# ScalarE sets up the two tap accumulators of a depthwise convolution; one tap fewer takes the product path

## What is computed

```python
def conv_module(u, buf, w_in, w_dw, b_dw, g_ln, b_ln, w_out):
    a, gl, z = jnp.split(u @ w_in, 3, axis=-1)
    v = a * jax.nn.sigmoid(gl)
    vp = jnp.concatenate([buf.astype(v.dtype), v], axis=1)
    y = lax.conv_general_dilated(vp, w_dw[:, None, :].astype(vp.dtype), window_strides=(1,),
                                 padding='VALID', dimension_numbers=('NWC', 'WIO', 'NWC'),
                                 feature_group_count=CONV_CH) + b_dw
    y = jax.nn.silu(layernorm(y, g_ln, b_ln))
    out = (y * jax.nn.silu(z)) @ w_out
```

## Time and profile before

| | |
|---|---|
| median of the three timed runs | 617.22 us |
| the profiled execution | 619.28 us |
| its span (first to last instruction) | 617.5 us |
| granted TensorE clock over the span | 0.969 of full |
| busy in the span: PE, DVE, ACT, POOL | 544.1, 438.5, 306.0, 299.6 us |
| from 51.5 to 178.3 us (126.8 us): PE, DVE, ACT, POOL | 121.89, 125.34, 66.25, 111.99 us |
| the same stretch: granted clock | 1.00 |
| 178.3 to 199.6 us (21.3 us): PE, DVE, ACT, POOL | 11.73, 19.18, 16.57, 13.18 us |

### The profile page before, as it was taken

One profiled execution on the slowest core, in us unless ns is written; L12 is line 12 of the kernel. 1 busy time (PEld: TensorE's weight loads), 2 busy tenths in 40 slices (PEclk: granted clock), 3 DMA queues, 4 the chain that ended last, 5 costly groups with the idle time before them and its releaser, 6 DMA issues.

```text
span 617.5 us, 10866 instructions
## 1 busy us (share of the span) xinstructions
PE 544.1 (88%) x4056; PEld 494.8 (80%) x4056; DVE 438.5 (71%) x848; ACT 306.0 (50%) x734; POOL 299.6 (49%) x275
## 2 busy tenths in 40 slices
PE   1899999988993899989999997899999998779981
PEld 0899999988772799879999996767877786479980
DVE  4886999999998848788387024766867867750066
ACT  6744456466466954644444334454455356354230
POOL 4748888889994931666729512011111112215033
PEclk9999999999998999999999998999999999969995
DMA  7423313331204400440313331200110121101012
GB/s 244 123 84 89 87 58 105 84 89 42 86 20 119 137 29 2 118 137 1 102 53 103 110 94 25 75 29 2 45 62 1 54 86 52 51 1 53 2 54 91
DMA packets 31397, 43.17 MB, mean 70 GB/s; under 512 B 5840, under 2 KB 21744, under 8 KB 31344
## 3 DMA queue, kind: packets, MB, share of 16 engines
q1 hardware_dynamic: 31344, 42.47, 23.2%
HBM read 37.25 MB, written 3.10 MB: 65 GB/s over the span
## 4 chain that ended last, share of the span: by engine, by line
PE 50%; DVE 32%; ACT 5%; issue 4%; SPq 3%; POOL 3%; DMA 2%; DVEq 0%; ACTq 0%
PE ps L429 13%; DVE ps L973 13%; PE ps L431 12%; PE ps L430 12%; PE ps L1675 3%; PE ps L1716 2%; DVE probs L1226 2%; PE ps L1696 2%; ACT probs L816 2%; SPq L492 2%; POOL rtop_lo L420 1%; DVE rowmax L1199 1%; DVE ps L900 1%; DVE zs L1278 1%; DVE xT L1281 1%
## 5 line engine op out<-in xcount | busy, mean ns | idle before, releaser
L420 POOL TENSOR_TENSOR rlow_lo<-stage,rlow_hi 128x384 fp32r<-128x384 f32 (+2 forms) x88 | 98.2, 1128 | 213.3 <-ACT rlow_hi L414 213.3
L429 PE MATMUL ps<-act_hi,rlow_hi 128*128 128x272 f32 (+1 forms) x368 | 110.4, 300 | 19.9 <-issue 8.8
L973 DVE SCALAR_TENSOR_TENSOR ps<-v,vecs,ps 128x574 f32<-128x574 f32 x162 | 118.4, 811 | 0.0
L429 PE MATMUL ps<-act_hi,rtop_hi 128*128 128x272 f32 x384 | 112.0, 292 | 3.6 <-DVE v L944 2.2
L431 PE MATMUL ps<-act_hi,rtop_lo 128*128 128x272 f32 x384 | 111.1, 289 | 0.0
L430 PE MATMUL ps<-act_lo,rtop_hi 128*128 128x272 f32 x384 | 110.5, 288 | 0.0
L431 PE MATMUL ps<-act_hi,rlow_lo 128*128 128x272 f32 (+1 forms) x368 | 107.1, 291 | 0.0
L430 PE MATMUL ps<-act_lo,rlow_hi 128*128 128x272 f32 (+1 forms) x368 | 106.9, 291 | 0.0
L429 PEld LDWEIGHTS ps<-act_hi,rlow_hi 128*128 128x128 f32 (+1 forms) x368 | 69.6, 189 | 23.9 <-issue 11.1
L429 PEld LDWEIGHTS ps<-act_hi,rtop_hi 128*128 128x128 f32 x384 | 72.2, 188 | 4.8 <-DVE v L944 2.7
L420 POOL TENSOR_TENSOR rtop_lo<-stage,rtop_hi 128x384 fp32r<-128x384 f32 (+1 forms) x56 | 64.4, 1168 | 23.7 <-ACT rtop_hi L414 23.7
(11 more groups left out here) (186 smaller groups left out, 1252.8 us busy)
## 6 DMA issues: line engine op xcount, KB each, us to landing
stage<-w_in SPq DMA_DIRECT2D x64, 192.0 KB, 2.6
stage<-w_bi SPq DMA_DIRECT2D x24, 256.0 KB, 2.7
stage<-w_ao SPq DMA_DIRECT2D x16, 256.0 KB, 2.9
stage<-w_bo SPq DMA_DIRECT2D x16, 256.0 KB, 2.8
stage<-w_qb SPq DMA_DIRECT2D x16, 192.0 KB, 2.6
xT<-x_t SPq DMA_DIRECT2D x4, 544.0 KB, 5.7
y_out<-xT SPq DMA_DIRECT2D x16, 136.0 KB, 1.8
stage<-w_kb SPq DMA_DIRECT2D x8, 256.0 KB, 2.7
```

The lines of the kernel that those rows point to most:

```text
L420: nc.gpsimd.tensor_tensor(l, stage[:, u % STAGES, 0:unit_cols(u)], h.bitcast(F32), ALU.subtract).then_inc(lo_done, 1)
L429: nc.tensor.matmul(out, wh, xh, start=start, stop=False)
L973: ins = nc.vector.scalar_tensor_tensor(out=dst, in0=src, scalar=tap, in1=dst, op0=ALU.mult, op1=ALU.add)
```

## The change

The tap split moves by one: six product taps instead of seven in tiles 0 to 6, so that 25 taps are DVE's side, and eleven instead of ten in tile 7, which leaves seven products there instead of eight. Taps 0 and 1 of DVE's side are no longer DVE instructions. ScalarE makes them (`acc_init`): first accumulator 1, when DVE's first sum of the tile before has read it, then accumulator 0 with the bias, when that tile is finished. DVE's loop starts at w = 2, with an accumulating step on accumulator 1, and waits on `acc_set`. In ScalarE's loop the order becomes: products 0 and 1, high parts 0 and 1, the two set-ups of tile c, the history copy, product 2; tile 0's set-ups stand behind its sigmoid. The accumulators move to banks of their own (4 and 5, 6 and 7; before, both had columns in bank 5), and so the first ones-matmul, whose output is in bank 7, now waits for the end of tile 7. The first sum becomes one instruction over all 574 columns.

```diff
-POOL_TAPS = 7
+POOL_TAPS = 6
 PADDS = POOL_TAPS - 1
-LAST_DVE_TAPS, PE_TAPS = 10, 13
+LAST_DVE_TAPS, PE_TAPS = 11, 13
...
+def dve_steps(j):
+
+    return tap_split(j)[0] - 2 + 1
...
-        acc = [flat[:, 4 * 512 + CCOLS * i:4 * 512 + CCOLS * i + CCOLS] for i in range(2)]
+        acc = [flat[:, (4 + 2 * i) * 512:(4 + 2 * i) * 512 + CCOLS] for i in range(2)]
...
+            def acc_init(j, w):
+
+                act.wait_ge(v_done, j + 1)
+                act.wait_ge(state_put, j + 1)
+                if j:
+                    if w == 1:
+                        act.wait_ge(tap_done, sum(dve_steps(i) for i in range(j)))
+                    else:
+                        act.wait_ge(y_ready, j)
+                tap = vecs[:, V_DW + WIDTH * j + w:V_DW + WIDTH * j + w + 1]
+                src = v[:, j % 2, w:w + CCOLS]
+                if w == 1:
+                    ins = nc.scalar.activation(acc[1], src, ACT.Copy, scale=tap)
+                else:
+                    ins = nc.scalar.activation(acc[0], src, ACT.Identity, bias=vecs[:, V_BDW + j:V_BDW + j + 1], scale=tap)
+                ins.then_inc(acc_set, 1)
...
                 products(0, 1)
+                units(0, 1)
+                if c >= 1:
+                    acc_init(c, 1)
+                    acc_init(c, 0)
                 if j < KD:
                     if j >= 2:
                         act.wait_ge(y_ready, j - 1)
                     nc.scalar.activation(v[:, j % 2, HIST + SEQ:2 * HIST + SEQ], state[:, j, :], ACT.Copy).then_inc(state_put, 1)
-                units(0, 1)
                 products(2)
...
+                if j == 0:
+                    acc_init(0, 1)
+                    acc_init(0, 0)
...
-                for w in range(taps):
+                for w in range(2, taps):
                     if not last and w == taps - (GLU_AHEAD if j + 2 < KD else LAST_GLU_AHEAD):
                         glu(j + 1)
-                    dst = acc[w % 2]
+                    dst = acc[(w + 1) % 2]
...
-                    if w == 0:
-                        ins = nc.vector.tensor_scalar(dst, src, tap, vecs[:, V_BDW + j:V_BDW + j + 1], ALU.mult, ALU.add)
-                    elif w == 1:
-                        ins = nc.vector.tensor_scalar(dst, src, tap, None, ALU.mult)
+                    if w < 4:
+                        dve.wait_ge(acc_set, 2 * j + w - 1)
                     else:
...
-                finish((rest[:, 0:SEQ], rest[:, SEQ + HIST:CCOLS]), acc[1], rest).then_inc(tap_done, 1)
+                nc.vector.tensor_tensor(rest, acc[1], rest, ALU.add).then_inc(tap_done, 1)
...
             pe.wait_ge(fold_done, folds(KD - 2))
+            pe.wait_ge(y_ready, KD)
             ysum(YMEAN[0], ysums[:, 0, blk(0)], True)
-            pe.wait_ge(y_ready, KD)
```

More of the change, by code:

```diff
@@ L295, in build @@
             sem("sig_done"), sem("z_evac"), sem("prod_done"), sem("ysq_done"), sem("gate_done"))
-        state_put, fold_done = sem("state_put"), sem("fold_done")
+        state_put, fold_done, acc_set = sem("state_put"), sem("fold_done"), sem("acc_set")
         diag_done = sem("diag_done")
@@ L960, in _ @@
                     dve.wait_ge(y_ready, j)
-                for w in range(taps):
+                for w in range(2, taps):
                     if not last and w == taps - (GLU_AHEAD if j + 2 < KD else LAST_GLU_AHEAD):
                         glu(j + 1)
-                    dst = acc[w % 2]
+                    dst = acc[(w + 1) % 2]
                     src = v[:, j % 2, w:w + CCOLS]
                     tap = vecs[:, V_DW + WIDTH * j + w:V_DW + WIDTH * j + w + 1]
-                    if w == 0:
-                        ins = nc.vector.tensor_scalar(dst, src, tap, vecs[:, V_BDW + j:V_BDW + j + 1], ALU.mult, ALU.add)
-                    elif w == 1:
-                        ins = nc.vector.tensor_scalar(dst, src, tap, None, ALU.mult)
+                    if w < 4:
+                        dve.wait_ge(acc_set, 2 * j + w - 1)
                     else:
                         dve.wait_ge(tap_done, taps_issued - 1)
-                        ins = nc.vector.scalar_tensor_tensor(out=dst, in0=src, scalar=tap, in1=dst,
-                                                             op0=ALU.mult, op1=ALU.add)
-                    ins.then_inc(tap_done, 1)
+                    nc.vector.scalar_tensor_tensor(out=dst, in0=src, scalar=tap, in1=dst,
+                                                   op0=ALU.mult, op1=ALU.add).then_inc(tap_done, 1)
                     taps_issued += 1
```

## The result

The changed kernel is slower: a median of 622.25 us over 20 runs against 618.28 us for 20 runs of the kernel before on the same chip, 4.0 us apart. The ratio over the runs is 1.0054 (95% interval 1.0039 to 1.0068), which is 3.3 us. The forecast was +1.1 us and "no difference", with 618.3 us and a range up to 621.5 us: too low in size, and the loss is clear of the noise. Of the 4.0 us between 622.25 and 618.3, 1.1 are not the change's, since the median of the kernel before is 618.28 us over twenty runs where three had given 617.22. The profiled execution has a span of 620.6 us against 617.5 before. In the two traces all of the loss lies ahead of the layer norm's reciprocal, which stands at 198.05 instead of 194.88; from there to the end both kernels take 422.6 us (620.6 - 198.05 and 617.5 - 194.88).

The account below looks back on a forecast made before the run. VectorE was taken to set the pace of tiles 1 to 7. +2.5 (first handover) - 4.6 (tile periods) + 0.5 (PE in tile 6) + 2.7 (the rest) = +1.1 us on 617.22 gave 618.3 us, range 614.5 to 621.5.

Parts of the forecast that it names:

- first handover: Tile 1's start: ScalarE's set-up queues behind a copy, products and high parts, so DVE begins at 60.95, losing 2.5 us.
- six tile periods, with the wait for PE in tile 6: Tiles 1 to 6: periods of 19.21 instead of 19.98 us gain 4.6 us, less 0.5 us waiting for PE.
- from tile 7's start to the reciprocal: Last tile and layer-norm statistics: order of the last tile and lateness of ScalarE and GpSimd cost 2.7 us.
- the first rival: Tile borders: late weight loads hold high parts ahead of each set-up; 619.1 us, or 621.5 at worst landings; chance 0.19.
- The last tile: Tile 7: products 2 to 6 wait behind the set-up, DVE waits 1.7 us for GpSimd, last sum at 185.15.
- The ones-matmul on them takes 0.62 us: Layer norm: after squares starting at 190.7, TensorE's matmul takes 0.62 us; first variance from 190.85 to about 191.85.
- The ysum moved behind the end of tile 7 costs nothing: Ahead of the layer norm: the moved ysum adds nothing, since it waits for the last fold and the squares end later.
- 4.03 us behind it: Layer norm: the reciprocal follows the first variance by 4.03 us, putting it at 195.9.
- End stays covered: Layer norm rival: DVE's 2.3 us gain at the last sum reaches the reciprocal, giving 614.9 us; chance 0.12.
- saving comes whole: Whole-convolution rival: the first handover is also not late, so 4.8 us are won, giving 612.4 us; chance 0.10.
- its two signs of being wrong: Borders 20 us apart with ScalarE waiting for weight DMAs, or the last sum at 183 or 184 with no wait.

Follow-up runs that it names:

- tile 1's set-up first: Changed kernel, but for tile 1 ScalarE sets the accumulators right behind the copy of z(1), ahead of two products and two high parts; ratio 1.0019 to the kernel before.
- the late set-up: Changed kernel, but ScalarE sets the last tile's two accumulators behind that tile's seven products instead of ahead of the last five; ratio 0.9996 to the kernel before.
- the run with TensorE kept busy: Changed kernel plus ten unread matmuls ahead of the layer norm's sums, the copy of z(7) swapped with one high part; ratio 1.0047 to the kernel before.

## Why the prediction was wrong

The mechanisms that it names were found in the trace. Two terms of its sum had the wrong size, both to the same side, and in the larger one two things stood at nothing: TensorE's matmuls at the lower clock, and VectorE's wait for GpSimd's late work. Term by term, against the trace of the changed kernel:

| term | forecast us | measured us |
|---|---|---|
| first handover (tile 1's start) | +2.5 | +2.73 |
| six tile periods, with the wait for PE in tile 6 | -4.1 | -3.26 |
| from tile 7's start to the reciprocal | +2.7 | +3.70 |
| sum at the reciprocal | +1.1 | +3.17 |

**First handover: right in size.** Set-ups of 0.73 and 0.82 us (0.74 and 0.84 forecast), first step at 61.16 instead of 60.95; 0.12 of the 0.21 is a later start of the convolution in this execution (33.12 against 33.00 us for the first product v). That the loss is "not shared with any other wait" was not right: with tile 1's set-up first, 0.63 of the 2.20 us won at tile 1 were gone at tile 7, behind TensorE's z(2).

**Tile periods: mis-sized by 0.83 us.** The forecast took 19.21 us for a steady period, and the six are 19.23, 19.73, 19.23, 19.30, 19.29 and, with the wait for TensorE, 19.81 (19.71 forecast). Of the miss 0.43 us is one border, tile 3's, where a load that landed 3.8 us after its issue held the high parts ahead of the set-up. That is the first rival's mechanism at one border of four and not at every one; the sum had put it at nothing. The execution with the late set-up shows no such wait, so it comes and goes. The rest is 0.02 to 0.10 us a border. The forecast had one wait of 0.05 us, for accumulator 0; the trace has two. The first step waits for accumulator 1 (a gap of 0.20 us where 0.14 stood before), which the text had ready in time, and the seventeen steps take 12.45 us instead of the 12.39 of tile 1, whose accumulator 0 was early: 0.06 us each.

**The last tile: right in kind.** Products behind the set-up, adds of 1.40 us, a wait of 2.01 us (1.7 forecast), last sum at 186.42 (1.27 behind the forecast 185.15, of which 1.05 are tile 7's own lateness), squares at 191.68 (190.7), high parts waiting for loads ahead of the root: all stand where the text put them. The late set-up proves the cause.

**Behind it: the step that failed.** "The ones-matmul on them takes 0.62 us", and "The ysum moved behind the end of tile 7 costs nothing: it waits for the last fold, and the squares end later still." The move itself cost nothing, as said: the folds end at 188.94, y of tile 7 at 188.82. But the folds were forecast late themselves, and with them TensorE stands 3.46 us instead of 1.62. Five pairs of ones-matmuls stand ahead of the one that needs the squares. At the pitch of 0.46 us they would have been through at about 191.4 (an estimate: 188.99, the first pair 0.54 as in the late set-up's trace, then four of 0.46), before the squares start at 191.68. With the clock at 0.50 until 192 they were through at 192.86, so TensorE and not the squares came last, and the variance follows 1.92 us behind the squares' start instead of 1.15: 0.8 us, of which the run with TensorE kept busy gives back 0.6.

The other step is "4.03 us behind it": VectorE's chain from the variance to the reciprocal took 4.45 us. Its last instruction took 0.77 instead of 0.30 us, and the rows of GpSimd beside it say why. In the kernel before, GpSimd stood from 193.85 on:

```profile
190.07 3.78 POOL L420 TENSOR_TENSOR rlow_lo<-stage,rlow_hi 128x512 fp32r<-128x512 f32 x3 [2.37 <-ACT rlow_hi L414]
...
194.66 0.30 DVE L1007 TENSOR_SCALAR var_b<-var_b 128x272 f32<-128x272 f32 x1
```

In the changed kernel its low parts last until 199.25:

```profile
188.89 10.36 POOL L425 TENSOR_TENSOR rlow_lo<-stage,rlow_hi 128x512 fp32r<-128x512 f32 x8
...
197.35 0.77 DVE L1032 TENSOR_SCALAR var_b<-var_b 128x272 f32<-128x272 f32 x1
```

The chain has two instructions whose inputs all lie in SBUF, the square of the mean (L1026) and this one, each run twice. In the ten traces of this case, forty times in all, they took 0.44 and 0.30 us where GpSimd stood when they started, or was in its last 0.12 us (ten times); in the other thirty they ended 0.29 to 0.31 and 0.15 to 0.17 us behind the end of the GpSimd instruction in which they started, however much of it was left. That is a wait for it. No run moves GpSimd's work alone, so the price of 0.4 us is read from these rows and not from a time. The prediction asked only whether GpSimd's own next work would feel its lateness.

So of the 2.15 us by which the reciprocal is later than the forecast 195.9, 1.05 lie at tile 7's start, 0.8 at TensorE, 0.4 behind the variance at VectorE beside GpSimd, and 0.1 go the other way in ScalarE's row.

**The cases and their chances.** "End stays covered" and "saving comes whole" fell as their own objections said. What the text never asked is the direction that the experiments show: the saving of 3.3 us on VectorE was there, and the order of one tile in one queue spent it. The forecast also kept the range's upper end to one cause (late loads at every border), while the miss was a sum of small ones with the same sign. Neither of its two signs of being wrong came: borders of 20 us and a last sum without a wait say nothing of TensorE and VectorE in the layer norm, where the miss was largest.

One price can be settled: by the Trainium skill, page "ScalarE: Activation LUTs", section "What ACT_TABLE_LOAD costs", the two set-ups would take about 0.757 and 0.850 us, an estimate from its figures for one and two pointer operands and 574 columns. The trace has 0.73 and 0.82, so the extra operand agrees (0.09 us). The product of the same width, with one such operand and into SBUF, has a mean of 0.765: the set-up into PSUM took some 0.03 us less.

## What to carry to other kernels

An instruction that moves to another in-order queue takes its wait along: ask what stands behind it that was ready, above all in the last round, where the next round no longer hides the delay; here the same instructions in another order were worth 3.6 us. When such a move makes TensorE stand, price what it does next at the lower clock as well as the wait; and when it makes an engine late, look at what the others do beside it, and not only at its own next work. And once the set-up is off the bottleneck engine, try the rest of the split again: with the order mended, the seventh product that the change had taken back to VectorE was worth another 0.6%.

## What the runs showed of the hardware

- The granted clock around TensorE's gap ahead of the layer norm, in stretches of 2 us: with gaps of 0.67, 0.75, 1.02, 1.48, 1.62 and 1.78 us it stayed at 1.00; with 3.46 us it fell to 0.65 and 0.50, with 3.48 us (tile 1's set-up first) to 0.62 and 0.53, two pairs of matmuls behind the end of the gap, with 5.29 us to 0.74 and 0.50, within the gap. At the lower clock the pitch of a pair of ones-matmuls was 0.9 instead of 0.46 us.
- ScalarE's set-up into PSUM, 574 columns, took 0.73 to 0.75 us with one and 0.82 to 0.84 with two vector operands; VectorE's with two took 0.88.
- GpSimd's add of 574 columns took 1.19 to 1.43 us, and 7.04 us for five in a row.
- The same VectorE instruction on 272 columns behind the variance, from SBUF to SBUF, took 0.30 us with GpSimd standing and 0.58 to 1.40 us when it started within a GpSimd instruction, whose end it outlasted by 0.15 to 0.17 us each time.
